# Dense gates of a routed expert layer from one-hot products: bf16 in three parts against rounded fp32 in two

## The chip, the cores and the metric

The kernel runs on one core of one Trainium2 chip. The metric is the device time of one execution in microseconds (us); the comparison goes by the median of several runs. The profile is of one execution, with a time of its own.

## The reference, cut to what matters

The kernel is a whole encoder block. What the change touches is the expert layer (PEER) at its end. Each of 512 tokens picks, for each of 8 heads, 16 experts out of 128 x 128, with a softmax gate on each:

```python
s_top, i_top = lax.top_k(s, PEER_TOPK)                    # two halves of 128 keys
cand = s_top[:, :, 0, :, None] + s_top[:, :, 1, None, :]
cand_idx = i_top[:, :, 0, :, None] * PEER_NKEYS + i_top[:, :, 1, None, :]
best_s, best_j = lax.top_k(cand.reshape(n, PEER_HEADS, -1), PEER_TOPK)
expert = jnp.take_along_axis(cand_idx.reshape(n, PEER_HEADS, -1), best_j, axis=-1)
gate = jax.nn.softmax(best_s, axis=-1)
h = jnp.einsum('nd,nhkd->nhk', xb, u[eb])
coef = gb * jax.nn.gelu(h, approximate=False)
out = jnp.einsum('nhk,nhkd->nd', coef, v[eb])
```

For 384 of the 512 tokens the kernel computes all 16384 experts densely and multiplies with a gate that is zero for experts that were not picked. So it needs, for each of these tokens, the dense 128 x 128 matrix of its gates: the sum over its 128 picks of gate x (one-hot of the first key) x (one-hot of the second key). The other 128 tokens fetch the rows of their picks instead.

## The kernel before, in words

The stages run one after the other, with a barrier of all engines between them: `project`, `attend`, `scan_chunks`, `join`, `route`, `experts`. The change lies in `route`.

`route` streams 104 weight tiles of 128 x 1024 fp32 from memory: 16 tiles of the query projection and 88 expert tiles (expert keys whose hidden values are computed early and parked in memory). Each tile is split in a high part (ScalarE, line 1669) and a low part (the difference), both written as fp32r, fp32 rounded for TensorE. GpSimd makes the low part for the first 56 tiles (line 1644), VectorE for the last 48 (`low`, line 1936). TensorE multiplies a tile in 24 products: 16 with the high part (line 1741), 8 with the low part (line 1745), each with 384 columns for an expert tile. ScalarE applies GELU (line 1675) and issues the store (line 1678).

Order of the stage: 48 tiles while VectorE ranks the scores (`rank`), then 8 tiles "between" (`BETWEEN`), in whose middle TensorE turns the picks over by transposes (line 1785) so that a token's 128 picks lie along the partitions; VectorE copies the three turned pieces (first key, second key, gate) out of PSUM (line 1908) and splits the gate into three bf16 parts (lines 1910 to 1916). Then come 24 lots of 16 tokens. A lot has two expert tiles and four "fours", each of 4 tokens. For a four, VectorE

- compares a count of 0 to 127 with the first key of each pick (line 1925, into `is_key`),
- compares it with the second key (line 1926, into `hot2`),
- multiplies `is_key` with each gate part (line 1929, into `hot1`).

TensorE then makes, for each of the 4 tokens, one product per gate part of 128 x 128 x 128, added up in PSUM (line 1798). ScalarE copies a four from PSUM into the lot (line 1714), and SP stores the lot, 1 MB, when its fours are copied. `hot1` and `hot2` are rings of `RING` = 4 fours: VectorE waits before a four until TensorE has done the four four places earlier (`four_done`).

Orders on the engines' queues within a lot n, all written out by hand:

- TensorE: expert tile, four 4n, four 4n+1, expert tile, four 4n+2, four 4n+3.
- VectorE: four 4n, four 4n+1, low half of the lot's second tile, four 4n+2, four 4n+3, low half of the next lot's first tile, one product of a gathered row (`dot_rows`, line 1969). Ahead of lot 0 stands the low half of its first tile.
- ScalarE: high half of the tile three ahead, GELU and store of the tile, two copies, and the same again.
- GpSimd: after its low halves, the gathers of 24 rows of the expert table, in a ring of 8.

Of the kernel before, what the change touches and what calls it, by code (L numbers as in the profile page):

```python
# [18 lines left out]
F32 = mybir.dt.float32  # L19
BF16 = mybir.dt.bfloat16  # L20
F32R = mybir.dt.float32r
U32 = mybir.dt.uint32
ALU = mybir.AluOpType
ACT = mybir.ActivationFunctionType
AX = mybir.AxisListType

P = 128
# [18 lines left out]
DENSE = SEQ - P  # L46
# [1489 lines left out]
def route(nc, a, g):  # L1536
# [4 lines left out]
    K = PEER_TOPK  # L1541
# [7 lines left out]
    FOUR = 4  # L1549
    FOURS = LOTS * LOT // FOUR  # L1550
    PARTS3 = 3
    RING = 4
    with ExitStack() as ctx:
# [5 lines left out]
        free = h1T.rearrange("p k t -> p (k t)")  # L1559
        act_out, qT = (free[:, 2048 + 1024 * x:3072 + 1024 * x].rearrange("p (j t) -> p j t", j=2) for x in range(2))  # L1560


        hot2 = sb("hot2", [P, RING, 2, P, 2], BF16)
        is_key = sb("is_key", [P, 2, 2, P, 2], BF16)
# [8 lines left out]
        gateT = sb("gateT", [P, DENSE])  # L1573

        gate_parts = sb("gate_parts", [P, FOURS, PARTS3, FOUR], BF16)
        picks_b = sb("picks_b", [P, 2, DENSE], BF16)
        small = sb("small", [P, NT * PEER_HEADS])
        count16, count128 = sb("count16", [P, K]), sb("count128", [P, P, 2], BF16)
# [8 lines left out]
        hot1 = sb("hot1", [P, RING, PARTS3, 2, P, 2], BF16)  # L1587
# [13 lines left out]
        gate_split, compared = sem("gate_split"), sem("compared")  # L1601
# [35 lines left out]
        @block.gpsimd  # L1637
        def _(pool):
            nc.gpsimd.iota(count16[:, :], [[1, K]], 0, 0, allow_small_or_imprecise_dtypes=True).then_inc(counted, 1)  # L1639
            nc.gpsimd.iota(count128[:, :, :], [[1, P], [0, 2]], 0, 0, allow_small_or_imprecise_dtypes=True).then_inc(counted, 1)  # L1640

            def low(s, j):
                pool.wait_ge(w_high, s + 1)
                nc.gpsimd.tensor_tensor(w_hl[:, j % RING, 1, :], staged[:, j % RING, :],  # L1644
                                        w_hl[:, j % RING, 0, :].bitcast(F32), ALU.subtract).then_inc(w_low, 1)

            with pool.Fori(0, BY_POOL // 8) as i:
                for j in range(8):
                    low(i * 8 + j, j)
            pool.wait_ge(gathering["picked"], 1)  # L1650
            for n in range(GATHERED_EARLY):
                gather_rows(nc, pool, a, gathering, n)

        @block.scalar
        def _(act):
# [50 lines left out]
            for j in range(BETWEEN):  # L1706
                expert(TOPK_TILES + j)
                if j == 1:
                    act.wait_ge(lowered, 1)
                    nc.scalar.activation(picks[:, 2], picks[:, 2], ACT.Exp).then_inc(raised, 1)  # L1710

# [18 lines left out]
        def _(pe):  # L1730
# [59 lines left out]
            def four(u):  # L1790

                q = u % 4
                if u >= 4:
                    pe.wait_ge(four_copied, u - 3)
                pe.wait_ge(hot_ready, u + 1)
                for n in range(FOUR):
                    for part in range(PARTS3):
                        last = nc.tensor.matmul(ps[:, 4 + q, P * n:P * (n + 1)], hot2[:, q, n // 2, :, n % 2],  # L1798
                                                hot1[:, q, part, n // 2, :, n % 2],
                                                start=(part == 0), stop=(part == PARTS3 - 1))  # L1800
                last.then_inc(four_done, 1)
# [8 lines left out]
        def _(dve):  # L1810
# [95 lines left out]
            for x in range(3):  # L1906
                dve.wait_ge(picks_turned, x + 1)
                v_.tensor_copy(gateT[:, :] if x == 2 else picks_b[:, x, :], ps[:, 4 + x, 0:DENSE]).then_inc(picks_copied, 1)
            dve.wait_ge(picks_copied, 3)
            by_four = gateT[:, :].rearrange("p (u n) -> p u n", n=FOUR)  # L1910
            for part in range(PARTS3):
                v_.tensor_copy(gate_parts[:, :, part, :], by_four).then_inc(gate_split, 1)
                dve.wait_ge(gate_split, 2 * part + 1)
                if part < PARTS3 - 1:
                    v_.tensor_tensor(by_four, by_four, gate_parts[:, :, part, :], ALU.subtract).then_inc(gate_split, 1)
                    dve.wait_ge(gate_split, 2 * part + 2)

            def four(u):

                r, now = u % RING, slice(FOUR * u, FOUR * (u + 1))  # L1920
                count = count128[:, :, :].unsqueeze(1).broadcast_to([P, 2, P, 2])
                pairs = lambda x: picks_b[:, x, now].rearrange("p (m n) -> p m n", n=2).unsqueeze(2).broadcast_to([P, 2, P, 2])
                if u >= RING:
                    dve.wait_ge(four_done, u - RING + 1)
                v_.tensor_tensor(is_key[:, u % 2], count, pairs(0), ALU.is_equal).then_inc(compared, 1)
                v_.tensor_tensor(hot2[:, r], count, pairs(1), ALU.is_equal)
                dve.wait_ge(compared, u + 1)
                part_pairs = gate_parts[:, u, :, :].rearrange("p c (m n) -> p (c m) n", n=2)
                v_.tensor_tensor(hot1[:, r].rearrange("p c m k n -> p (c m) k n"),
                                 is_key[:, u % 2].unsqueeze(1).broadcast_to([P, PARTS3, 2, P, 2]),  # L1930
                                 part_pairs.unsqueeze(2).broadcast_to([P, 2 * PARTS3, P, 2]), ALU.mult
# [368 lines left out]
```

## Time and profile before

| | |
|---|---|
| Time, median of 3 runs | 2092.43 us (2092.4 to 2100.97) |
| Profiled execution: its time, its span | 2092.4 us, 2090.7 us |
| Busy over the span: TensorE, VectorE | 91%, 74% |
| Busy over the span: ScalarE, GpSimd | 36%, 27% |
| Lots of `route`, first to last four on TensorE | 1067.33 to 1334.75 us |
| Mean granted TensorE clock over the span | 0.946 of full speed |

The profile names engines PE (TensorE products), PEld (TensorE weight loads, which overlap PE), DVE (VectorE), ACT (ScalarE), POOL (GpSimd) and SP (SyncE). L1929 is line 1929 of the kernel. Times are from the start of the span. Records of one engine may overlap the next by a little, since it is pipelined, so the cadence is read from starts and not from durations. "[0.21 <-PE ps L1798]" behind a row is idle time of that engine before it, and who ended it. A row with a count merges instructions of one kind in a row. DMA rows marked SPq or ACTq are issues of those queues.

### The profile page before, as it was taken

What the parts mean: (1) busy time and instruction counts of PE and PEld (TensorE: products, weight loads), DVE (VectorE), ACT (ScalarE), POOL (GpSimd) and SP (SyncE); (2) the same over time, 40 slices, a digit from 0 to 9 for tenths busy, and PEclk for the clock granted to TensorE, in tenths of its full rate; (3) what the DMA queues carried; (4) which work ended last, traced back from release to release, by engine and by line L of the source; (5) the groups of instructions that cost most, each with busy time, mean ns of one, the idle gap of its engine ahead of it and who ended that gap; (6) DMA issues with size and microseconds to landing.
All of it is one profiled execution on the core that took longest, in us unless ns stands there. A gap on an engine that the chain in (4) does not pass through costs nothing. (4 is left out here: it accounts for less than half of the span.)

```text
span 2090.7 us, 33958 instructions
## 1 busy us (share of the span) xinstructions
PE 1903.4 (91%) x13250; PEld 1622.2 (78%) x13250; DVE 1538.9 (74%) x2834; ACT 755.0 (36%) x1113; POOL 569.9 (27%) x395
## 2 busy tenths in 40 slices
PE   6989998879999879999499999579999999999996
PEld 4968876349874459999499999558888889999995
DVE  6278993414545369999978888368888887999998
ACT  3232454532220033433246656323333333333332
POOL 2322343000000045555221000112222225566660
PEclk9988998987999989999799999789999999999998
DMA  3211231010022044444277776599999998999992
GB/s 124 72 60 51 86 115 61 0 41 3 4 98 105 0 145 137 140 132 132 67 274 262 267 270 216 217 325 367 339 367 347 350 360 301 358 392 386 385 404 103
DMA packets 169686, 411.02 MB, mean 197 GB/s; under 512 B 13504, under 2 KB 85184, under 8 KB 166352
## 3 DMA queue, kind: packets, MB, share of 16 engines
q1 hardware_dynamic: 117712, 253.41, 35.2%
q0 software_dynamic: 36864, 134.23, 16.8%
q10 hardware_dynamic: 14976, 21.50, 2.8%
q8 instruction: 95, 1.56, 0.3%
q14 instruction: 39, 0.32, 0.0%
HBM read 360.33 MB, written 48.76 MB: 196 GB/s over the span
## 5 line engine op out<-in xcount | busy, mean ns | idle before, releaser
L2143 PE MATMUL ps<-v_hl,coef_hl 128*128 128x512 f32 x2304 | 535.9, 392 | 40.5 <-DVE coef_hl L2182 40.5
L2143 PEld LDWEIGHTS ps<-v_hl,coef_hl 128*128 128x128 f32 x2304 | 434.7, 189 | 131.4 <-DVE coef_hl L2182 42.0
L1741 PE MATMUL ps<-h_hl,w_hl 128*128 128x384 f32 (+1 forms) x1664 | 329.6, 350 | 8.7 <-DVE h_hl L1814 8.7
L1741 PEld LDWEIGHTS ps<-h_hl,w_hl 128*128 128x128 f32 x1664 | 294.8, 190 | 20.2 <-issue 9.1
L1959 POOL DMA_INDIRECT gathered_rows<-in_u_rows,pick_index x128 | 136.2, 1064 | 574.0 <-DVE pick_hidden L1969 465.3
L2087 ACT ACTIVATE v_hl<-v_staged 128x1024 fp32r<-128x1024 f32 x128 | 135.4, 1057 | 254.6 <-PE ps L2143 195.3
L2187 DVE TENSOR_TENSOR v_hl<-v_staged,v_hl 128x1024 fp32r<-128x1024 f32 x128 | 156.4, 1222 | 68.8 <-ACT v_hl L2087 68.8
L1959 POOL DMA_INDIRECT gathered_rows<-in_v,pick_index x128 | 176.0, 1375 | 105.6 <-DVE h_tok L1978 75.1
L1644 POOL TENSOR_TENSOR w_hl<-w_staged,w_hl 128x1024 fp32r<-128x1024 f32 x56 | 142.7, 2551 | 151.9 <-ACT w_hl L1669 151.6
L1978 DVE SCALAR_TENSOR_TENSOR h_tok<-gathered_rows,pick_hidden,h_tok 128x1024 f32<-128x1024 f32 x128 | 164.1, 1282 | 10.4 <-DVE h_tok L1978 0.5
L633 PE MATMUL ps<-hT_hl,w_hl 128*128 128x264 f32 (+1 forms) x1024 | 168.4, 323 | 0.0
L1745 PE MATMUL ps<-h_hl,w_hl 128*128 128x384 f32 (+1 forms) x832 | 168.1, 343 | 0.0
L633 PEld LDWEIGHTS ps<-hT_hl,w_hl 128*128 128x128 f32 x1024 | 150.9, 198 | 14.4 <-issue 2.8
L298 POOL TENSOR_TENSOR w_hl<-w_staged,w_hl 128x1024 fp32r<-128x1024 f32 x40 | 102.9, 2573 | 213.8 <-ACT w_hl L481 213.8
L1969 DVE CUSTOM_DVE_ANT_0 gathered_rows<-gathered_rows,h_tok 128x1024 f32<-128x1024 f32 x128 | 155.0, 1217 | 0.0
L1745 PEld LDWEIGHTS ps<-h_hl,w_hl 128*128 128x128 f32 x832 | 147.3, 188 | 5.0
L2093 ACT ACTIVATE coef_hl<-coef 128x384 fp32r<-128x384 f32 x128 | 65.7, 514 | 172.8 <-DVE coef L2178 172.8
L1669 ACT ACTIVATE w_hl<-w_staged 128x1024 fp32r<-128x1024 f32 x104 | 110.6, 1065 | 38.9 <-DMA w_staged<-in_stream 22.0
L2129 PE MATMUL ps<-h_hl,u_hl 128*128 128x384 f32 x640 | 118.4, 336 | 0.0
L2129 PEld LDWEIGHTS ps<-h_hl,u_hl 128*128 128x128 f32 x640 | 113.1, 188 | 3.1
L1639 POOL IOTA count<- 128x16 f32 x1 | 0.1, 149 | 398.3 <-POOLq L111 398.3
L1714 ACT ACTIVATE lot<-ps 128x512 f32<-128x512 f32 x96 | 95.9, 1105 | 19.9 <-PE ps L1798 19.9
(320 smaller groups left out, 2780.1 us busy)
## 6 DMA issues: line engine op xcount, KB each, us to landing
v_staged<-in_v SPq DMA_DIRECT2D x128, 512.0 KB
w_staged<-in_stream SPq DMA_DIRECT2D x104, 512.0 KB
dense_gates<-lot SPq DMA_DIRECT2D x24, 1024.0 KB
gates<-dense_gates SPq DMA_DIRECT2D x16, 1536.0 KB
w_staged<-in_w_in_t SPq DMA_DIRECT2D x40, 512.0 KB
h1T<-in_stream SPq DMA_DIRECT2D x40, 512.0 KB
parked_gelu<-h1T ACTq DMA_DIRECT2D x88, 192.0 KB, 2.5
coef<-parked_gelu SPq DMA_DIRECT2D x88, 192.0 KB
```

The source lines that it names most:

```text
L633: nc.tensor.matmul(banks[b], w_hl[:, j, 0, P * k:P * (k + 1)], hT_hl[:, part, k, lo:hi], start=(k == 0 and part == 0), stop=False)
L1644: nc.gpsimd.tensor_tensor(w_hl[:, j % RING, 1, :], staged[:, j % RING, :], w_hl[:, j % RING, 0, :].bitcast(F32), ALU.subtract).then_inc(w_ ...
L1669: nc.scalar.activation(w_hl[:, j % RING, 0, :], staged[:, j % RING, :], ACT.Copy).then_inc(w_high, 1)
L1741: nc.tensor.matmul(bank, w_hl[:, j % RING, 0, P * k:P * (k + 1)], h_hl[:, part, k, lo:hi], start=(k == 0 and part == 0), stop=False)
L1745: last = nc.tensor.matmul(bank, w_hl[:, j % RING, 1, P * k:P * (k + 1)], h_hl[:, 0, k, lo:hi], start=False, stop=(k == KD - 1))
L1959: nc.gpsimd.indirect_dma_start(gathering["rows"][:, slot, :], None, table, bass.IndirectOffsetOnAxis(gathering["index"][:, column:column + ...
L1969: nc.vector.tensor_tensor_reduce(rows, rows, h_tok[:, 0, :], 1.0, 0.0, ALU.mult, ALU.add, gathering["hidden"][:, n:n + 1]).then_inc(gather ...
L1978: nc.vector.scalar_tensor_tensor(h_tok[:, 0, :], gathering["rows"][:, slot, :], gathering["hidden"][:, pick:pick + 1], h_tok[:, 0, :], ALU ...
L2087: nc.scalar.activation(v_hl[:, k % HLS, 0, :], v_staged[:, k % STAGED, :], ACT.Copy).then_inc(v_high, 1)
L2129: nc.tensor.matmul(bank, u_hl[:, f % 2, 0, P * c:P * (c + 1)], h_hl[:, part, c, SEQ - DENSE:SEQ], start=(c == 0 and part == 0), stop=False)
L2143: last = nc.tensor.matmul(ps[:, 2 + 2 * t + half, :], coef_hl[:, k % HLS, c, P * t:P * (t + 1)], v_hl[:, k % HLS, v, 512 * half:512 * (hal ...
L2187: v_.tensor_tensor(v_hl[:, k % HLS, 1, :], v_staged[:, k % STAGED, :], v_hl[:, k % HLS, 0, :].bitcast(F32), ALU.subtract).then_inc(v_low, 1)
```

## The change

The three bf16 parts of the gate become two fp32r parts, high and low, and the one-hot tiles become fp32r too. `hot1` (3 parts) becomes `hot1_hl` (2 parts). The layout in pairs (`P, 2` innermost) is given up for a plain `[FOUR, P]`, so the key and the gate are now broadcast along the innermost dimension. A four has 8 products instead of 12. The high part of the gate is made by ScalarE, in its queue behind the tiles between, and VectorE waits for it (`gate_high`), subtracts and waits for that (`gate_low`) before its first low half. `is_key` moves into free room of `h1T`.

```diff
+        is_key = free[:, 0:2 * FOUR * P].rearrange("p (r n k) -> p r n k", r=2, n=FOUR)
-        hot2 = sb("hot2", [P, RING, 2, P, 2], BF16)
-        is_key = sb("is_key", [P, 2, 2, P, 2], BF16)
+        hot2 = sb("hot2", [P, RING, FOUR, P], F32R)
-        gateT = sb("gateT", [P, DENSE])
-        gate_parts = sb("gate_parts", [P, FOURS, PARTS3, FOUR], BF16)
-        picks_b = sb("picks_b", [P, 2, DENSE], BF16)
+        picksT = sb("picksT", [P, 3, DENSE])
+        gate_hl = sb("gate_hl", [P, 2, DENSE], F32R)
-        count16, count128 = sb("count16", [P, K]), sb("count128", [P, P, 2], BF16)
+        count16, count128 = sb("count16", [P, K]), sb("count128", [P, P])
-        hot1 = sb("hot1", [P, RING, PARTS3, 2, P, 2], BF16)
+        hot1_hl = sb("hot1_hl", [P, RING, 2, FOUR, P], F32R)
...
         # ScalarE, behind the loop over the tiles between
+            act.wait_ge(picks_copied, 3)
+            nc.scalar.activation(gate_hl[:, 0, :], picksT[:, 2, :], ACT.Copy).then_inc(gate_high, 1)
...
         # TensorE, in four(u)
-                    for part in range(PARTS3):
-                        last = nc.tensor.matmul(ps[:, 4 + q, P * n:P * (n + 1)], hot2[:, q, n // 2, :, n % 2],
-                                                hot1[:, q, part, n // 2, :, n % 2],
-                                                start=(part == 0), stop=(part == PARTS3 - 1))
+                    for part in range(2):
+                        last = nc.tensor.matmul(ps[:, 4 + q, P * n:P * (n + 1)], hot2[:, q, n, :],
+                                                hot1_hl[:, q, part, n, :], start=(part == 0), stop=(part == 1))
...
         # VectorE
-                v_.tensor_copy(gateT[:, :] if x == 2 else picks_b[:, x, :], ps[:, 4 + x, 0:DENSE]).then_inc(picks_copied, 1)
+                v_.tensor_copy(picksT[:, x, :], ps[:, 4 + x, 0:DENSE]).then_inc(picks_copied, 1)
             dve.wait_ge(picks_copied, 3)
-            by_four = gateT[:, :].rearrange("p (u n) -> p u n", n=FOUR)
-            for part in range(PARTS3):
-                v_.tensor_copy(gate_parts[:, :, part, :], by_four).then_inc(gate_split, 1)
-                dve.wait_ge(gate_split, 2 * part + 1)
-                if part < PARTS3 - 1:
-                    v_.tensor_tensor(by_four, by_four, gate_parts[:, :, part, :], ALU.subtract).then_inc(gate_split, 1)
-                    dve.wait_ge(gate_split, 2 * part + 2)
+            dve.wait_ge(gate_high, 1)
+            v_.tensor_tensor(gate_hl[:, 1, :], picksT[:, 2, :], gate_hl[:, 0, :].bitcast(F32), ALU.subtract
+                             ).then_inc(gate_low, 1)
+            dve.wait_ge(gate_low, 1)
...
-                v_.tensor_tensor(is_key[:, u % 2], count, pairs(0), ALU.is_equal).then_inc(compared, 1)
-                v_.tensor_tensor(hot2[:, r], count, pairs(1), ALU.is_equal)
+                v_.tensor_tensor(is_key[:, u % 2], count, picksT[:, 0, now].unsqueeze(2).broadcast_to([P, FOUR, P]),
+                                 ALU.is_equal).then_inc(compared, 1)
+                v_.tensor_tensor(hot2[:, r], count, picksT[:, 1, now].unsqueeze(2).broadcast_to([P, FOUR, P]), ALU.is_equal)
                 dve.wait_ge(compared, u + 1)
-                v_.tensor_tensor(hot1[:, r].rearrange("p c m k n -> p (c m) k n"),
-                                 is_key[:, u % 2].unsqueeze(1).broadcast_to([P, PARTS3, 2, P, 2]),
-                                 part_pairs.unsqueeze(2).broadcast_to([P, 2 * PARTS3, P, 2]), ALU.mult
+                v_.tensor_tensor(hot1_hl[:, r], is_key[:, u % 2].unsqueeze(1).broadcast_to([P, 2, FOUR, P]),
+                                 gate_hl[:, :, now].bitcast(F32).unsqueeze(3).broadcast_to([P, 2, FOUR, P]), ALU.mult
                                  ).then_inc(hot_ready, 1)
```

## Rows read from the trace of the kernel before

**Rows 1.** Busy time by engine over the lots; then PEclk, DMA share, GB/s.
```profile
1067.33:1334.75 267.42, 267.42 (x2281) 260.02 (x2280) 223.10 (x367) 159.75 (x187) 17.70 (x15) 1.00 0.70 241
```

**Rows 2.** Timeline of one lot: start, length, engine, line, operation.
```profile
1178.88 1.22 DVE L1936 TENSOR_TENSOR w_hl<-w_staged,w_hl 128x1024 fp32r<-128x1024 f32 x1
1180.01 1.22 DVE L1969 CUSTOM_DVE_ANT_0 gathered_rows<-gathered_rows,h_tok 128x1024 f32<-128x1024 f32 x1
1180.53 1.40 PEld L1798 LDWEIGHTS ps<-hot 128*128 128x128 bf16 x24 [0.16 <-issue]
1181.45 0.43 DVE L1925 TENSOR_TENSOR is_key<-count,picks_b 128x512 bf16<-128x512 bf16 x1 [0.21 <-PE ps L1798]
1181.79 0.42 DVE L1926 TENSOR_TENSOR hot<-count,picks_b 128x512 bf16<-128x512 bf16 x1
1181.89 2.76 PEld L1741 LDWEIGHTS ps<-h_hl,w_hl 128*128 128x128 f32 x16
1182.12 0.95 DVE L1929 TENSOR_TENSOR hot<-is_key,gate_parts 128x1536 bf16<-128x1536 bf16 x1
1182.99 0.42 DVE L1925 TENSOR_TENSOR is_key<-count,picks_b 128x512 bf16<-128x512 bf16 x1
...
1186.19 1.40 PEld L1798 LDWEIGHTS ps<-hot 128*128 128x128 bf16 x24 [0.16 <-issue]
1187.11 0.43 DVE L1925 TENSOR_TENSOR is_key<-count,picks_b 128x512 bf16<-128x512 bf16 x1 [1.36 <-PE ps L1798]
```

**Rows 3.** Groups by line in the lots: busy us, mean ns | idle before.
```profile
L1929 DVE TENSOR_TENSOR hot<-is_key,gate_parts 128x1536 bf16<-128x1536 bf16 x92 | 87.4, 950 | 0.0
L1798 PEld LDWEIGHTS ps<-hot 128*128 128x128 bf16 x1152 | 67.1, 97 | 7.5 <-issue 7.5
L1936 DVE TENSOR_TENSOR w_hl<-w_staged,w_hl 128x1024 fp32r<-128x1024 f32 x45 | 54.7, 1216 | 0.0
L1925 DVE TENSOR_TENSOR is_key<-count,picks_b 128x512 bf16<-128x512 bf16 x92 | 38.8, 421 | 40.3 <-PE ps L1798 40.3
L1926 DVE TENSOR_TENSOR hot<-count,picks_b 128x512 bf16<-128x512 bf16 x92 | 38.4, 417 | 0.0
```

**Rows 4.** Four-byte vector operations elsewhere, by line: ns min/median/max.
```profile
L1814 DVE TENSOR_TENSOR h_hl<-h1T,h_hl x8: 681/682/691, 753.3 to 757.5; 128x512 fp32r<-128x512 f32 x8
...
L1862 DVE TENSOR_TENSOR cand<-top x8: 1210/1212/1218, 795.7 to 1020.3; 128x1024 f32<-128x1024 f32 x8
...
L1876 DVE TENSOR_TENSOR is_place<-place,count x16: 1210/1226/3429, 806.6 to 1031.4; 128x1024 f32<-128x1024 f32 x16
```

**Rows 5.** Weight loads of 64 and of 128 fp32 columns, by line.
```profile
L1205 PEld LDWEIGHTS ps<-inv,low x256: 129/135/136, 498.7 to 597.0; 64*64 64x64 f32 x128
...
L1755 PEld LDWEIGHTS ps<-sub_keys,h1T x128: 187/192/192, 776.4 to 983.8; 128*128 128x128 f32 x128
```

**Rows 6.** Timelines of TensorE in two other stages, for the cadence of its products.
```profile
60.56 4.09 PE L633 MATMUL ps<-hT_hl,w_hl 128*128 128x264 f32 x32
64.49 2.12 PE L638 MATMUL ps<-hT_hl,w_hl 128*128 128x264 f32 x16
...
776.59 1.95 PE L1755 MATMUL ps<-sub_keys,h1T 128*128 x16
778.29 1.99 PE L1741 MATMUL ps<-h_hl,w_hl 128*128 128x384 f32 x10
```

**Rows 7.** Timeline ahead of the first lot.
```profile
1046.27 2.44 DVE L1912 CAST gate_parts<-gateT 128x384 bf16<-128x384 f32 x1
...
1053.02 1.23 DVE L1936 TENSOR_TENSOR w_hl<-w_staged,w_hl 128x1024 fp32r<-128x1024 f32 x1 [2.08 <-ACT w_hl L1669]
1063.37 0.49 ACT L1675 ACTIVATE h1T<-ps 128x384 f32<-128x384 f32 x1 [2.14 <-PE ps L1745]
1063.89 0.34 ACTq L1678 DMA_DIRECT2D parked_gelu<-h1T  x1
```

**Rows 8.** Timeline of TensorE's last four products.
```profile
1333.36 1.57 PE L1798 MATMUL ps<-hot 128*128 128x128 bf16 x24
```

More of the change, by code:

```diff
@@ L1550, in route @@
     FOURS = LOTS * LOT // FOUR
-    PARTS3 = 3
     RING = 4
@@ L1600, in route @@
             sem(n) for n in ("lowered", "raised", "gates_ready", "picks_turned", "picks_copied"))
-        gate_split, compared = sem("gate_split"), sem("compared")
+        gate_high, gate_low, compared = sem("gate_high"), sem("gate_low"), sem("compared")
         hot_ready, four_done, four_copied = sem("hot_ready"), sem("four_done"), sem("four_copied")
@@ L1639, in _ @@
             nc.gpsimd.iota(count16[:, :], [[1, K]], 0, 0, allow_small_or_imprecise_dtypes=True).then_inc(counted, 1)
-            nc.gpsimd.iota(count128[:, :, :], [[1, P], [0, 2]], 0, 0, allow_small_or_imprecise_dtypes=True).then_inc(counted, 1)
+            nc.gpsimd.iota(count128[:, :], [[1, P]], 0, 0, allow_small_or_imprecise_dtypes=True).then_inc(counted, 1)
             def low(s, j):
@@ L1918, in four @@
+            v_.tensor_tensor(gate_hl[:, 1, :], picksT[:, 2, :], gate_hl[:, 0, :].bitcast(F32), ALU.subtract
+                             ).then_inc(gate_low, 1)
+            dve.wait_ge(gate_low, 1)
             def four(u):
                 r, now = u % RING, slice(FOUR * u, FOUR * (u + 1))
-                count = count128[:, :, :].unsqueeze(1).broadcast_to([P, 2, P, 2])
-                pairs = lambda x: picks_b[:, x, now].rearrange("p (m n) -> p m n", n=2).unsqueeze(2).broadcast_to([P, 2, P, 2])
+                count = count128[:, :].unsqueeze(1).broadcast_to([P, FOUR, P])
@@ L1927, in four @@
                 dve.wait_ge(compared, u + 1)
-                part_pairs = gate_parts[:, u, :, :].rearrange("p c (m n) -> p (c m) n", n=2)
-                v_.tensor_tensor(hot1[:, r].rearrange("p c m k n -> p (c m) k n"),
-                                 is_key[:, u % 2].unsqueeze(1).broadcast_to([P, PARTS3, 2, P, 2]),
-                                 part_pairs.unsqueeze(2).broadcast_to([P, 2 * PARTS3, P, 2]), ALU.mult
+                v_.tensor_tensor(hot1_hl[:, r], is_key[:, u % 2].unsqueeze(1).broadcast_to([P, 2, FOUR, P]),
+                                 gate_hl[:, :, now].bitcast(F32).unsqueeze(3).broadcast_to([P, 2, FOUR, P]), ALU.mult
```

## Prediction

> **What bounds the kernel now.** I began with the page: its sum rows say where the engines are busy but not which of them sets the pace in the stretch that the diff touches, so I looked for the stretch itself. The loop of 24 lots runs from 1067.33 us, when the first one-hot product starts, to 1334.75. In it TensorE is busy for the whole stretch, VectorE for 83% of it, ScalarE for 60%, at full clock [rows 1]. The timeline of one lot shows the same as a cadence: a half lot is one expert tile (24 products of 384 columns) and two fours (24 products of 128 columns), and repeats after 5.66 us, for instance from 1180.53 to 1186.19. Weight loads of the tile start at 1181.89, those of the next fours at 1186.19 after a gap of 0.16, so the tile takes 4.14 us (172.5 ns a product) and the two fours 1.36 us (57 ns a product) [rows 2]. A lot is 11.32 us. VectorE waits for TensorE in every half lot, 0.21 and 1.36 us, because the ring of four hot tiles is full; TensorE waits for nobody [rows 2, 3]. So TensorE bounds this stage, and VectorE follows with a slack of 1.57 us in 11.32. That slack is the number on which the change depends.
>
> **VectorE, the term that decides.** One four is now 421 + 417 + 950 ns for 512, 512 and 1536 two-byte elements [rows 3]. Their successors start 0.34, 0.33 and 0.87 us later: each record overlaps the next by some 0.085 us, and a four has a cadence of 1.54 us [rows 2]. After the change it is 512, 512 and 1024 elements of four bytes. The trace has these: the four-byte operation on 512 elements takes 682 ns, on 1024 elements 1210 to 1218; with both operands broadcast (the candidate sums) it is 1212, and a comparison with an innermost broadcast has the same minimum, 1210 [rows 4]. The output type with rounding costs nothing extra, since the low half of a weight tile, written that way, takes 1216 [rows 3]. So the elements pass at 1.04 ns each instead of 0.52, and two thirds of the third operation's elements at twice the time is more. A four becomes 682 + 682 + 1216 = 2580 ns against 1788: +0.79 us, cadence 2.33.
>
> A lot on VectorE is four fours, two low halves at 1.13 (1178.88 to 1180.01) and a row product at 1.22. Now 6.16 + 2.26 + 1.22 = 9.64, plus 1.57 of waiting, leaves 0.11 of small gaps in 11.32. Then: 9.32 + 2.26 + 1.22 + 0.11 = 12.91 us. VectorE alone needs 1.59 us more per lot than the lot takes now.
>
> **TensorE, the term without a row.** The products fall from 12 to 8 a four, but become single-pass four-byte products with 128 moving columns, of which the trace has none. From below: such products with 264 and 384 columns come every 122.8 ns (32 in 3.93 us) and 172.5 ns, which is a column per 2.4 GHz clock plus 13 ns [rows 2, 6]; so 53.3 + 12.7 = 66 ns. From the middle: a weight load of 128 four-byte columns has a record of 188 to 192 ns, one of 64 columns 135, so 0.84 ns a column and 107 ns for 128 beside a fixed part; the two-byte load of 128 columns is 97 in all [rows 3, 5]. Behind 264 or more columns such a load is hidden, behind 128 it isn't. From above: the ordinary four-byte product of 128 columns gives two records, 106 ns apart (16 in 1.70 us), 213 ns a product [rows 5, 6]; with the 13 ns added, 226. I take 107, since the weight-load records are of the very type and width that the change uses, and an unhidden load is the only thing in them that differs from the longer products. The Trainium skill, TensorE: Matmul & The Clock Gate, section Weight-path perf modes, says that the fast weight load is on for 128 weights of any type but FP32; with that page's load of one column per 1.2 GHz cycle (section LDWEIGHTS) the load would be 107 ns, against 66 if one went by the longer products alone. The trace's 0.84 ns a column agrees with it, but no run of before shows the pair with 128 columns.
>
> A half lot on TensorE is then 4.14 + 0.16 + 16 products: 5.36 us with 66 ns, 6.01 with 107, 7.71 with 213, 7.92 with 226; a lot 10.7, 12.0, 15.4 or 15.8 us. Up to 107, and even at 120 (12.4), VectorE with 12.91 is the slower engine, and the price of a product doesn't enter the sum.
>
> **Start and end.** Removed are the five gate splits, from 1046.27 to the wait that ends at 1053.02. They are hidden: in that wait VectorE stands 2.08 us for ScalarE anyway [rows 7], so they return nothing. The three copies from PSUM stay. Added are one ScalarE copy of 384 elements and one subtraction on VectorE (384 elements: 682 less 128 x 1.04 = 0.55 us). The copy stands in ScalarE's queue behind the last tile of the eight between, whose GELU ends at 1063.86, its store's issue at 1064.2 [rows 7]; the copy ends near 1064.8 (0.5 us), the subtraction near 1065.5. Queued behind that wait on VectorE are the first low half, and all fours. TensorE's tile now waits for that low half: it wants it at 1067.33 - 0.16 - 1.38 (8 of 24 products) = 1065.8. The low half ends near 1066.7, TensorE loses some 0.9 us, and VectorE, which had its first four fours done before 1067, starts its first only at 1066.7. It thus loses its whole lead of four fours.
>
> From there VectorE runs without a stop: TensorE has finished each ring slot long before VectorE wants it again. 24 lots of 12.91 less the low half and the row product that stand behind the last four (2.35) end at 1066.7 + 309.8 - 2.35 = 1374.2. With 0.1 to finish, 0.9 for the last eight products and 0.2 of flush it is 1375.4, against 1334.9 now (1333.36 + 1.57) [rows 8]: +40.5 us. ScalarE's work per lot is unchanged, 6.9 us of 12.9, and so is what follows the stage: the same buffers and the same first transfers, later by that much. Nothing of the later stages runs ahead, as they begin behind a barrier. The profiled execution took 2092.4 us, 1.7 more than its span and equal to the median of the runs; 2092.4 + 40.5 = 2133.
>
> **Rivals.**
> A. Products with 128 columns take the four-pass rate, 213 to 226 ns. For it: the only four-byte products with such short rows show it. Against: those are of the plain type and leave two records each, while the rounded type leaves one at 264 columns and above. TensorE is then the bound: fours 0 and 1 are ready at 1069.0 and 1071.4, the second ends at 1073.1, and 47 half lots of 7.71 to 7.92 follow: 1435.5 to 1445.3, so +100 to +110, 2193 to 2203 us. The Trainium skill, FP8 and Floating Point Precision, section TensorE Precision Notes, keeps four passes for true FP32 and lets the reduced form be truncated on reading, which speaks against this rival; no row has the case.
> B. An exposed weight load and the product don't overlap: 107 + 53 = 160 ns. A half lot is 6.86; 1072.7 + 47 x 6.86 = 1395.1, +60, 2152 us. Against it: the plain product's records, with loads of the same 188 to 192 ns, are only 106 apart [rows 5, 6].
> C. Faster: the four-byte vector operations keep a cadence under the TensorE lot, and TensorE gains from 8 products at 66 ns instead of 12 at 57. It decides when a four is under 1.93 us (11.32 less 3.48 and 0.11, over four); then a lot falls towards 10.72, 24 x 0.6 = 14 us less, 2078. Against it are all rows of group 4, which give 2.33.
> D. The slack covers it all: no change. The same point, 1.93 us a four, with 107 ns on TensorE would make lots of 12.0 and so still +16; only a price between 66 and 85 ns gives no change.
>
> **How the numbers follow.** My forecast (VectorE bound, any TensorE price up to 120 ns) gets 0.62, B 0.08, A 0.25, C 0.03, D 0.02. The forecast's own range is 2124 to 2142: 0.4 us a lot either way for gaps on VectorE. Leaving out A would leave out a quarter, so the range reaches to it: 2124 to 2204. A measurement of this kernel can tell about 0.5% (10 us) from nothing; by these cases 0.03 faster, 0.02 within it, 0.95 slower.
>
> **What would show it.** In the lots: comparisons of about 682 ns twice and a multiplication of 1216, VectorE busy without waits for the products, lots of 12.9 us; TensorE waiting for the hot tiles; 8 products a four at 107 ns, weight loads of 188 to 192. The first comparison near 1066.7, the last product near 1375. Rival A shows products over 200 ns apart and VectorE still waiting; B 160. I am wrong if the four-byte comparison with its stride-zero operands is not one element per 1.04 ns, or if TensorE, idle for a moment in each lot, loses its granted clock, as the rows at 1.00 don't show [rows 1].

## The result

| | median | lowest to highest | runs |
|---|---|---|---|
| before | 2092.41 us | 2091.73 to 2100.97 | 4 |
| changed | 2131.38 us | 2130.43 to 2132.12 | 4 |

The change costs 39.0 us: the ratio is 1.0176, with a 95% interval of 1.015 to 1.0203. A second set of the same kernel, run on one chip with three of the experiments, gave 2129.12 us against 2092.47, ratio 1.017 (1.0129 to 1.0212). 2133 us was forecast, slower.

The profiled execution of the changed kernel took 2135.26 us, span 2133.5, some 4 us over its median. A shift of 6.1 us is there before `route` has begun (the first low half of its activations starts at 759.4 us, at 753.3 in the profile of before [rows 4]), in stages whose code is unchanged. So I compare `route` from that instruction on: to the start of the last product it takes 581.4 us before and 618.6 after, 37.2 more. From there to the end of the span it is 756.0 and 755.5 us. The whole of the change lies in `route`. A second profiled execution of the changed kernel has the same 618.6 us there (754.8 to 1373.4).

### The profile page after: what moved, and what is told of

The parts are those of the page before. It is cut to its first block and busy times, and to the rows that moved or that the text cites. A ratio compares the mean times of both kernels' runs of the same rounds, so it can differ in the third digit from the quotient of the medians.

```text
span 2133.5 us, 33188 instructions
## 1 busy us (share of the span) xinstructions
PE 1929.4 (90%) x12866; PEld 1648.7 (77%) x12866; DVE 1608.0 (75%) x2830; ACT 757.5 (36%) x1114; POOL 567.8 (27%) x395
## 5 line engine op out<-in xcount | busy, mean ns | idle before, releaser
L1922 DVE TENSOR_TENSOR hot_hl<-h1T,gate_hl 128x1024 fp32r<-128x1024 f32 x96 | 117.2, 1220 | 0.0
```

Of the source, the lines that this page charges most:

```text
L1922: v_.tensor_tensor(hot1_hl[:, r], is_key[:, u % 2].unsqueeze(1).broadcast_to([P, 2, FOUR, P]), gate_hl[:, :, now].bitcast(F32).unsqueeze(3 ...
```

## The profile after

Busy time by engine from the first four to the last (columns as in [rows 1]: PE, PEld, DVE, ACT, POOL, then the granted clock, DMA share, GB/s):

```profile
1075.01:1378.31 303.30, 288.75 (x1896) 286.23 (x1896) 303.08 (x380) 161.38 (x186) 18.33 (x16) 0.99 0.62 214
```

[Rows 1] had TensorE busy for the whole of 267.42 us and VectorE for 223.10. Now VectorE is busy for the whole of 303.30 and TensorE for 288.75. The bound has changed engines.

The groups by line in the lots (busy us, mean ns, idle time before and its releaser), the answers to [rows 3]:

```profile
L1922 DVE TENSOR_TENSOR hot_hl<-h1T,gate_hl 128x1024 fp32r<-128x1024 f32 x96 | 117.2, 1220 | 0.0
L1796 PE MATMUL ps<-hot_hl,hot 128*128 128x128 f32 x768 | 95.8, 273 | 15.2 <-DVE hot_hl L1922 15.2
L1796 PEld LDWEIGHTS ps<-hot_hl,hot 128*128 128x128 f32 x768 | 94.6, 192 | 17.9 <-issue 15.6 <-DVE hot_hl L1922 2.4
...
L1918 DVE TENSOR_TENSOR h1T<-count,picksT 128x512 f32<-128x512 f32 x96 | 66.0, 687 | 0.0
L1920 DVE TENSOR_TENSOR hot<-count,picksT 128x512 fp32r<-128x512 f32 x96 | 65.9, 687 | 0.0
L1928 DVE TENSOR_TENSOR w_hl<-w_staged,w_hl 128x1024 fp32r<-128x1024 f32 x48 | 58.6, 1220 | 0.0
```

The waits have changed sides. The comparison `is_key` waited 40.3 us for products [rows 3] and now waits 0.0; the products wait 15.2 us for `hot1_hl`. (The name h1T in these rows is where `is_key` lies now.) A four on VectorE is 687 + 687 + 1220 = 2594 ns, where 421 + 417 + 950 = 1788 stood [rows 3].

One lot of the timeline, from VectorE's and the weight loads' side (start, length), the answer to [rows 2]:

```profile
1180.55 0.68 DVE L1918 TENSOR_TENSOR h1T<-count,picksT 128x512 f32<-128x512 f32 x1
...
1182.89 0.68 DVE L1918 TENSOR_TENSOR h1T<-count,picksT 128x512 f32<-128x512 f32 x1
...
1184.61 1.92 PEld L1796 LDWEIGHTS ps<-hot_hl,hot 128*128 128x128 f32 x16
...
1185.23 1.22 DVE L1928 TENSOR_TENSOR w_hl<-w_staged,w_hl 128x1024 fp32r<-128x1024 f32 x1
...
1186.37 1.22 DVE L1961 CUSTOM_DVE_ANT_0 gathered_rows<-gathered_rows,h_tok 128x1024 f32<-128x1024 f32 x1
1186.45 2.73 PEld L1739 LDWEIGHTS ps<-h_hl,w_hl 128*128 128x128 f32 x16
...
1187.51 0.08 DVE L1961 DVE_READ_ACCUMULATOR2_ANT pick_hidden<- 128x1 f32 x1
1187.51 0.69 DVE L1918 TENSOR_TENSOR h1T<-count,picksT 128x512 f32<-128x512 f32 x1
...
1192.39 0.97 PEld L1796 LDWEIGHTS ps<-hot_hl,hot 128*128 128x128 f32 x8 [0.80 <-issue]
1192.42 1.08 PE L1796 MATMUL ps<-hot_hl,hot 128*128 128x128 f32 x8 [0.69 <-DVE hot_hl L1922]
...
1193.33 0.68 DVE L1918 TENSOR_TENSOR h1T<-count,picksT 128x512 f32<-128x512 f32 x1
```

The same place in the lot is reached at 1180.55 and 1193.33: a lot is 12.78 us (11.32 before). A four takes 2.34 (1180.55 to 1182.89), and nothing on VectorE has idle time ahead of it. TensorE waits once a lot, 0.69 us before the second four. Sixteen products of two fours take 1.84 us (1184.61 to 1186.45, load to load), 115 ns each where twelve and twelve took 57 each.

Ahead of the first lot:

```profile
1070.16 0.53 ACT L1708 ACTIVATE gate_hl<-picksT 128x384 fp32r<-128x384 f32 x1 [0.41 <-ACT h1T L1671]
...
1070.79 0.56 DVE L1908 TENSOR_TENSOR gate_hl<-picksT,gate_hl 128x384 fp32r<-128x384 f32 x1 [18.61 <-ACT gate_hl L1708]
1071.39 1.23 DVE L1928 TENSOR_TENSOR w_hl<-w_staged,w_hl 128x1024 fp32r<-128x1024 f32 x1
1072.53 0.69 DVE L1918 TENSOR_TENSOR h1T<-count,picksT 128x512 f32<-128x512 f32 x1
1072.66 1.34 PEld L1743 LDWEIGHTS ps<-h_hl,w_hl 128*128 128x128 f32 x8 [0.99 <-DVE w_hl L1928]
```

VectorE stands idle for 18.61 us for the gate's high part, and TensorE's weight loads for the tile then wait 0.99 us for its low half. The first comparison starts at 1072.53, less the shift of 6.1 at 1066.4.

TensorE's granted clock just behind these waits, and the tile that ran then:

```profile
1078.90:1082.00 3.10, 3.10 (x11) 3.10 (x11) 3.10 (x6) 1.94 (x2) 0.00 (x0) 0.50 0.54 169
...
1090.00:1378.30 288.30, 274.98 (x1827) 272.61 (x1825) 288.09 (x362) 155.00 (x179) 17.19 (x15) 1.00 0.64 219
```
```profile
1077.35 1.91 PE L1796 MATMUL ps<-hot_hl,hot 128*128 128x128 f32 x8 [1.23 <-DVE hot_hl L1922]
1079.06 5.39 PE L1739 MATMUL ps<-h_hl,w_hl 128*128 128x384 f32 x16
1084.28 1.58 PE L1743 MATMUL ps<-h_hl,w_hl 128*128 128x384 f32 x8
```

TensorE's products had waited 0.67, 0.68 and 1.23 us within 6 us. Behind that the granted clock read 0.50, the level of 1.2 GHz, and the 16 products of a tile took 5.22 us (1079.06 to 1084.28) where they take 2.83 at 1.00 (1180.56 to 1183.39). It cost nothing here, since VectorE had no idle time in these lots. From 1090 on, with one wait of 0.69 us a lot, the clock read 1.00.

## The experiments

All but the two with bf16 parts are edits of the changed kernel. The profiled lots are the sharper measure, since the timed runs of one kernel spread by up to 17 us in some sets. In the profiled executions the stages ahead of `route`, whose code is the same in all of them, end at different times: the first low half of the activations starts between 747.9 and 759.4 us.

### What bounds the lots: fewer products, less multiplication, more products

`high_products_only`:

```diff
-                    for part in range(2):
+                    for part in range(1):
                         last = nc.tensor.matmul(ps[:, 4 + q, P * n:P * (n + 1)], hot2[:, q, n, :],
-                                                hot1_hl[:, q, part, n, :], start=(part == 0), stop=(part == 1))
+                                                hot1_hl[:, q, part, n, :], start=True, stop=True)
```

> The changed kernel with four products a four instead of eight: only the high gate part is multiplied in, the low part is made on VectorE but left out of the sum. If VectorE bounds the lots (my theory), nothing moves: about 2131 us, lots still 12.8 us, TensorE only waits longer. If TensorE with its products (115 ns apart in the trace of after) sets the pace, 96 x 4 x 0.115 = 44 us go: about 2087.

Busy time over its lots:

```profile
1061.70:1364.50 302.80, 258.84 (x1512) 253.28 (x1512) 302.80 (x379) 161.83 (x186) 18.32 (x16) 0.95 0.62 214
```

TensorE is busy for 29.9 us less (288.75 to 258.84) and the lots are as long as before: 302.8 us against 303.3. (The products taken out were worth some 44 us at 115 ns each. TensorE's mean granted clock in these lots is 0.95 instead of 0.99, which makes an estimate of 0.04 x 303 = 12 us by which the rest took longer.) VectorE is busy in all of them. From the first low half (747.9) to the last product (1364.0) it is 616.1 us, 618.6 in the changed kernel. The time is 2134.26 us (2121.17 to 2138.21), ratio 1.0215 (1.0187 to 1.0243): no gain. That half of TensorE's new products weigh nothing is shown. The ratio even lies above that of the changed kernel, while the profiled execution is the fastest of the set, with the earliest start of `route` of all (747.9 us). The three slower ones have a lower mean clock (0.940 and 0.935 twice, against 0.943); they were not profiled, so the cause stays open.

`high_multiply_only`:

```diff
-                v_.tensor_tensor(hot1_hl[:, r], is_key[:, u % 2].unsqueeze(1).broadcast_to([P, 2, FOUR, P]),
-                                 gate_hl[:, :, now].bitcast(F32).unsqueeze(3).broadcast_to([P, 2, FOUR, P]), ALU.mult
+                v_.tensor_tensor(hot1_hl[:, r, 0], is_key[:, u % 2],
+                                 gate_hl[:, 0, now].bitcast(F32).unsqueeze(2).broadcast_to([P, FOUR, P]), ALU.mult
...
-                                                hot1_hl[:, q, part, n, :], start=(part == 0), stop=(part == 1))
+                                                hot1_hl[:, q, 0, n, :], start=(part == 0), stop=(part == 1))
```

> The changed kernel with VectorE multiplying the high part alone (512 elements instead of 1024); the eight products stay, both with the high part, so the low part is left out. VectorE's four falls from 2.33 to 1.80 us, its lot from 12.8 to 10.7. If VectorE bounds the lots, they fall until TensorE does, 2 x (4.14 + 0.16 + 16 x 0.115) = 12.3 us: 24 x 0.5 = 12 us less, about 2119. If TensorE already bounds them, no change, 2131.

Busy time over its lots, and weight loads of one half lot in its timeline:

```profile
1062.60:1346.00 283.40, 281.71 (x1896) 281.43 (x1896) 254.96 (x380) 160.97 (x188) 18.85 (x16) 1.00 0.66 230
```
```profile
1182.40 1.92 PEld L1796 LDWEIGHTS ps<-hot_hl,hot 128*128 128x128 f32 x16
1184.24 2.73 PEld L1739 LDWEIGHTS ps<-h_hl,w_hl 128*128 128x128 f32 x16
```

The time falls to 2107.81 us (2100.49 to 2117.09), ratio 1.0094 (1.0058 to 1.0131). 512 elements less a four, on VectorE alone, take back half of the change by the medians and 23.3 of its 37.2 us in the trace. That is the direction expected with VectorE as the bound, and the rival (TensorE bound) is excluded. The size was wrong: 12 us were expected, 1.0176 to 1.0094 is 17, and in the trace (749.4 to 1344.7, 595.3 us) it is 23.3. TensorE bounds these lots, but at a half lot of 5.94 us, not the 6.14 of the expectation: 1.84 for the products and 4.11 for the tile, without the 0.16 us that stood ahead of the fours in [rows 2]. In this kernel 24 x (12.78 - 5.94 x 2) = 21.6 us is the VectorE part of the change, and 24 x (11.88 - 11.32) = 13 us the part that TensorE would charge if VectorE cost nothing.

`twelve_products`:

```diff
-                    for part in range(2):
+                    for x, part in enumerate((0, 1, 1)):
                         last = nc.tensor.matmul(ps[:, 4 + q, P * n:P * (n + 1)], hot2[:, q, n, :],
-                                                hot1_hl[:, q, part, n, :], start=(part == 0), stop=(part == 1))
+                                                hot1_hl[:, q, part, n, :], start=(x == 0), stop=(x == 2))
```

> The changed kernel with 12 products a four, the low part multiplied in twice. It doubles as a test of TensorE's price and of where it would take over. With 115 ns a product, as the trace of after has it, a half lot on TensorE is 4.11 + 24 x 0.115 = 6.87 us, a lot 13.7, above VectorE's 12.8: 24 x 0.96 = 23 us more than the changed kernel. At 107 ns it is 14 us more, at 66 ns nothing.

Busy time over its lots, and its weight loads:

```profile
1065.70:1392.00 326.30, 324.61 (x2280) 324.33 (x2280) 304.45 (x380) 165.46 (x187) 18.33 (x16) 1.00 0.58 199
```
```profile
1182.94 2.82 PEld L1796 LDWEIGHTS ps<-hot_hl,hot 128*128 128x128 f32 x24
1185.67 2.73 PEld L1739 LDWEIGHTS ps<-h_hl,w_hl 128*128 128x128 f32 x16
...
1189.78 2.82 PEld L1796 LDWEIGHTS ps<-hot_hl,hot 128*128 128x128 f32 x24
```

2152.26 us against 2129.12 for the changed kernel on the same chip: +23.1, as expected. In the trace, from the first low half (752.0) to the last product (1390.8), it is 20.2 more. Half lots are 6.84 us (1182.94 to 1189.78), 24 products take 2.73 (114 ns each), and TensorE is again busy nearly from end to end. The two engines cross at (6.39 - 4.11) / 0.114 = 20 products a half lot, 10 a four (6.39 is half of VectorE's lot).

### Why such a product costs 112 to 115 ns

`wide_products` (first) and `narrow_weights` (second), one run each:

```diff
                 for n in range(FOUR):
-                    for part in range(2):
-                        last = nc.tensor.matmul(ps[:, 4 + q, P * n:P * (n + 1)], hot2[:, q, n, :],
-                                                hot1_hl[:, q, part, n, :], start=(part == 0), stop=(part == 1))
+                    last = nc.tensor.matmul(ps[:, 4 + q, 2 * P * (n % 2):2 * P * (n % 2 + 1)], hot2[:, q, n, :],
+                                            hot1_hl[:, q, n // 2, 2 * (n % 2):2 * (n % 2) + 2, :], start=True, stop=True)
```
```diff
-                        last = nc.tensor.matmul(ps[:, 4 + q, P * n:P * (n + 1)], hot2[:, q, n, :],
+                        last = nc.tensor.matmul(ps[0:64, 4 + q, P * n:P * (n + 1)], hot2[:, q, n, 0:64],
```

> The changed kernel with four products of 256 columns a four instead of eight of 128 (two tokens' halves side by side, so the sums over the parts are left out). A look at the cadence in the trace. If a product of 128 columns is bound by its weight load, one of 256 costs about the same, 107 to 120 ns, and two fours take 0.95 us instead of 1.84. If the moving columns set the price at 0.9 ns each, one of 256 takes 230 ns and two fours stay at 1.84. The lots stay at 12.8 us in both cases, VectorE being the bound.

> The changed kernel with weight loads of 64 columns instead of 128 (keys 64 to 127 of the second half are left out); still 8 products of 128 moving columns. If the weight load binds, the cadence falls from 115 ns to that of the moving columns, 53 + 13 = 66 ns, and two fours take about 1.06 us. If the moving columns bind, it stays at 115. The lots stay at 12.8 us.

One four in the timeline of `wide_products`, and one in that of `narrow_weights`:

```profile
1191.07 0.61 PE L1795 MATMUL ps<-hot_hl,hot 128*128 128x256 f32 x4
```
```profile
1188.20 0.64 PE L1796 MATMUL ps<-hot_hl,hot 128*64 128x128 f32 x8
```

A merged row runs from the first start to the last end, so the mean cadence, the time from one start to the next, is its length less one record, over the count less one. With 256 moving columns (a record is 279 ns) it is (610 - 279) / 3 = 110 ns; with 64 weight columns (record 223) it is (640 - 223) / 7 = 60 ns. In the changed kernel the product of 128 by 128 (record 274) stands at (1000 - 274) / 7 = 104 ns in a group of eight, 1.00 us long, and at (1900 - 274) / 15 = 108 in a group of 16. These two means are low because the second product of such a group starts only 57 ns after the first; the eight further products of the longer group cost (1900 - 1000) / 8 = 112 ns each. Over all lots the median from start to start is 112 ns with 128 by 128, 118 with 256 moving columns and 60 with 64 weight columns. So twice the moving columns cost at most some 6 ns, and half the weight columns save about 50. The load of 128 four-byte weight columns sets the price, as the middle estimate had it. With 64 weight columns the 60 ns are close to the 57 of the bf16 product, which has the same 128 moving columns, so there the load need no longer be what sets it. Both kernels took what the changed one takes (2128.81 and 2125.58 us, one run each), since VectorE sets the lots.

### The start: the gate's high part made earlier

```diff
             for j in range(BETWEEN):
...
+                if j == 3:
+                    act.wait_ge(picks_copied, 3)
+                    nc.scalar.activation(gate_hl[:, 0, :], picksT[:, 2, :], ACT.Copy).then_inc(gate_high, 1)
-            act.wait_ge(picks_copied, 3)
-            nc.scalar.activation(gate_hl[:, 0, :], picksT[:, 2, :], ACT.Copy).then_inc(gate_high, 1)
```

> The changed kernel with ScalarE's copy of the gate's high part moved ahead, right behind the fourth tile between instead of behind the eighth. My step on the start: VectorE makes its first four fours before TensorE wants them, and starts the fifth when the first is done, some 11 us earlier than now (1068.3 instead of 1066.6 + 12.8, in times of the profile of before); being the bound it keeps that: about 2120.5 us. Rival: the lead is used up in waits on the ring or is hidden by TensorE's tiles, less than 2 us of gain, 2130.

Its timeline, VectorE:

```profile
1043.52 0.56 DVE L1909 TENSOR_TENSOR gate_hl<-picksT,gate_hl 128x384 fp32r<-128x384 f32 x1 [0.67 <-ACT gate_hl L1709]
1048.92 1.23 DVE L1929 TENSOR_TENSOR w_hl<-w_staged,w_hl 128x1024 fp32r<-128x1024 f32 x1 [4.85 <-ACT w_hl L1665]
1050.07 0.69 DVE L1919 TENSOR_TENSOR h1T<-count,picksT 128x512 f32<-128x512 f32 x1
...
1064.28 0.69 DVE L1919 TENSOR_TENSOR h1T<-count,picksT 128x512 f32<-128x512 f32 x1 [1.32 <-PE ps L1797]
```

The wait of 18.61 us is 0.67. VectorE has four fours ready, waits once for the ring (1.32 us), and then keeps its lead as the bound. From the first low half (751.3) to the last product (1357.1) it is 605.8 us: 12.8 less than the changed kernel. 2115.3 us, ratio 1.0123 (1.01 to 1.0145) where the changed kernel had 1.0176 and 1.017: about 10 us. So the place of one ScalarE copy of 0.53 us carries a quarter to a third of the whole change.

### The number of products without the change of type

```diff
 (in the kernel before)
-    PARTS3 = 3
+    PARTS3 = 2
```

> The kernel before with two bf16 parts of the gate instead of three (the third, the last 8 bits of the gate, is left out): the saving in the number of products alone, without the change of type. TensorE bounds the lots there, so each half lot should lose 8 products of 57 ns: 48 x 0.45 = 22 us less, about 2071. VectorE's four falls to 1.27 us. Rival: the transfers (DMA busy 0.70 to 0.79 of the lots) or ScalarE's copies stop the fall; then 2075 to 2092.

> The kernel before with two bf16 parts instead of three, once more and in more rounds, since its first time had an interval of 11 us: 48 half lots of 5.19 instead of 5.66 us are 22.6 us less, a ratio of 0.989.

Weight loads in the timeline of the second set:

```profile
1180.08 0.93 PEld L1798 LDWEIGHTS ps<-hot 128*128 128x128 bf16 x16 [0.16 <-issue]
...
1185.28 0.93 PEld L1798 LDWEIGHTS ps<-hot 128*128 128x128 bf16 x16 [0.16 <-issue]
```

A half lot is 5.20 us. The first set gave a ratio of 0.9909 (0.9883 to 0.9935), the second 0.9889 (0.9864 to 0.9914), 2068.09 us against 2091.76. In the traces, from the first low half to the last product, it is 22.5 us less than before in the first set (756.6 to 1315.5) and 17.8 in the second (752.0 to 1315.6). In the second, TensorE's weight loads stood three times for the high half of a tile, once for 2.27 us:

```profile
1214.45 2.75 PEld L1741 LDWEIGHTS ps<-h_hl,w_hl 128*128 128x128 f32 x16 [2.27 <-ACT w_hl L1669]
```

The three are 4.8 us, and ScalarE, which makes the high halves, waited 57.0 us in 21 waits for transfers of the weight tiles. So the rival of the expectation, the transfers, begins to bind. The eight products a four that the change wanted are worth 18 to 23 us, if they keep the two-byte type. (VectorE multiplies 512 elements less a four too, but it had slack already.) This version beats both kernels; what it gives up is the third part of the gate, so that the gate has the 16 leading bits of its fraction instead of 24.

### Can VectorE get a part of it back?

`bf16_is_key` makes the first comparison in pairs and in bf16, as before, and multiplies in two instructions:

```diff
+                pairs = keys_b[:, now].rearrange("p (m n) -> p m n", n=2).unsqueeze(2).broadcast_to([P, 2, P, 2])
+                v_.tensor_tensor(is_key[:, u % 2], count_b[:, :, :].unsqueeze(1).broadcast_to([P, 2, P, 2]), pairs,
+                                 ALU.is_equal).then_inc(compared, 1)
...
+                for c in range(2):
+                    last = v_.tensor_tensor(hot1_hl[:, r, c].rearrange("p (m n) k -> p m k n", n=2), is_key[:, u % 2],
+                                            gate_hl[:, c, now].bitcast(F32).rearrange("p (m n) -> p m n", n=2).unsqueeze(2)
+                                            .broadcast_to([P, 2, P, 2]), ALU.mult)
+                last.then_inc(hot_ready, 1)
```

> The changed kernel with the first comparison in bf16 and in pairs, as before, and the multiplication in two instructions of 512 elements that read it beside the fp32 gate. VectorE's four: 0.34 + 0.60 + 1.20 = 2.14 us instead of 2.33, its lot 12.0 against TensorE's 11.9: some 18 us less than the changed kernel, 20 to 21 over the kernel before. If VectorE's time isn't what sets the lots, nothing changes. If an operation that mixes two-byte and four-byte operands costs more than 1.04 ns an element, less comes back.

It was a miss: 2171.03 us, ratio 1.038 (1.0347 to 1.0412), 42 us slower than the changed kernel. The comparison cost 422 ns as wanted, the multiplications 1089 each instead of the 682 that a four-byte operation on 512 elements takes. Two things had come together in them, mixed operand types and a write with 512 bytes between neighbouring elements, and two further kernels took them apart: `mixed_plain` only makes `is_key` bf16, `paired_fp32` only takes the paired layout, all in fp32.

```diff
 (mixed_plain)
-        is_key = free[:, 0:2 * FOUR * P].rearrange("p (r n k) -> p r n k", r=2, n=FOUR)
+        is_key = free[:, 0:FOUR * P].bitcast(BF16).rearrange("p (r n k) -> p r n k", r=2, n=FOUR)
```
```diff
 (paired_fp32)
-        is_key = free[:, 0:2 * FOUR * P].rearrange("p (r n k) -> p r n k", r=2, n=FOUR)
+        is_key = free[:, 0:2 * FOUR * P].rearrange("p (r m k n) -> p r m k n", r=2, m=2, n=2)
...
+                paired = lambda x: x.rearrange("p (m n) -> p m n", n=2).unsqueeze(2).broadcast_to([P, 2, P, 2])
+                v_.tensor_tensor(is_key[:, u % 2], count128[:, :].unsqueeze(1).unsqueeze(3).broadcast_to([P, 2, P, 2]),
+                                 paired(picksT[:, 0, now]), ALU.is_equal).then_inc(compared, 1)
...
+                for c in range(2):
+                    last = v_.tensor_tensor(hot1_hl[:, r, c].rearrange("p (m n) k -> p m k n", n=2), is_key[:, u % 2],
+                                            paired(gate_hl[:, c, now].bitcast(F32)), ALU.mult)
+                last.then_inc(hot_ready, 1)
```

> The changed kernel with is_key written as bf16 and everything else as it is: the multiplication reads a bf16 and an fp32 operand, in the plain layout. It separates the two things that came together in bf16_is_key, whose multiplications of 512 elements took 1089 ns instead of 682. If mixing two-byte and four-byte operands is what costs (1.84 ns an element), the multiplication takes some 2030 ns, a lot 3.3 us more, the kernel 78 us more than the changed one: about 2208. If the paired layout was the cause, it stays at 1216 ns and the kernel at 2130.

> The changed kernel with is_key in fp32 but in pairs, and the multiplication in two instructions that write with 512 bytes between neighbouring elements. If that write pattern is what made the 1089 ns, they take 1089 each here too, a four 3.0 us, and the kernel some 65 us more than the changed one, about 2195. If mixing the types was the cause, they take 682 ns each and the kernel is 6 us slower than the changed one, for the extra instruction: about 2136.

The multiplication in `bf16_is_key`, in `mixed_plain` and in `paired_fp32` (ns min/median/max, first and last start):

```profile
L1926 DVE TENSOR_TENSOR hot_hl<-h1T,gate_hl x192: 1031/1087/1152, 1063.2 to 1411.9; 128x512 fp32r<-128x512 bf16 x192
```
```profile
L1922 DVE TENSOR_TENSOR hot_hl<-h1T,gate_hl x96: 1215/1222/1228, 1064.1 to 1366.1; 128x1024 fp32r<-128x1024 bf16 x96
```
```profile
L1924 DVE TENSOR_TENSOR hot_hl<-h1T,gate_hl x192: 1045/1112/1209, 1072.8 to 1441.3; 128x512 fp32r<-128x512 f32 x192
```

Mixing costs nothing (1222 ns for 1024 elements, 2124.99 us). The layout is the cause: 1112 ns for 512 elements in pure fp32, 2199.16 us, one run each. And of the layout it is the write. The first comparison of `paired_fp32` reads in the same pairs but writes element by element in a row, and it costs what the plain second comparison beside it costs:

```profile
L1919 DVE TENSOR_TENSOR h1T<-count,picksT 128x512 f32<-128x512 f32 x75 | 53.1, 708 | 0.0
L1921 DVE TENSOR_TENSOR hot<-count,picksT 128x512 fp32r<-128x512 f32 x75 | 52.9, 706 | 0.0
...
1181.56 2.02 DVE L1924 TENSOR_TENSOR hot_hl<-h1T,gate_hl 128x512 fp32r<-128x512 f32 x2
1183.42 0.68 DVE L1919 TENSOR_TENSOR h1T<-count,picksT 128x512 f32<-128x512 f32 x1
```

The records overstate it a little: two multiplications take 1.86 us from start to start (1181.56 to 1183.42), 0.93 each. The slower two are changes on VectorE alone, and the end moved by their size: a four takes 2.77 us in `bf16_is_key` and 3.06 in `paired_fp32` instead of 2.34, so 96 x 0.43 = 41 and 96 x 0.72 = 69 us were to come, and 42 and 70 came (2171.03 and 2199.16 against 2129.12; in the traces, from the first low half to the last product, 45 and 66, and in the first of them VectorE also waited 4.9 us for a gathered row). That is two more signs of VectorE as the bound.

## Why the prediction was right, by its own steps

- **TensorE bounds the lots before, VectorE after.** Right. Taking TensorE work out of the changed kernel gained nothing, taking VectorE work out gained at once, and the idle time went over from one to the other.
- **A four on VectorE of 682 + 682 + 1216 ns.** Measured 687, 687, 1220, with a cadence of 2.34 us (2.33 forecast). The rows of other operations with the same element count and broadcast operands held for the new ones.
- **A lot of 12.91 us.** 12.78. The term that was mis-sized is the rest: the row product costs 1.14 (1186.37 to 1187.51), not 1.22, and the 0.11 us of gaps are gone, which fits that they stood beside waits for TensorE that no longer happen. 24 x 0.13 = 3.1 us is nearly all of the 3.3 by which the forecast for the stage was high (40.5 against 37.2).
- **The start.** First comparison forecast near 1066.7, found at 1066.4 after taking off the shift; TensorE's wait for the low half forecast at 0.9, found at 0.99 on the weight loads. The loss of the lead was folded into the sum; by itself it is 10 to 13 us, by `gate_copy_early`.
- **The removed gate splits return nothing.** Consistent with the trace, where VectorE waits for the gate's high part in their place, longer than they took; no run tried it by itself.
- **107 ns a product.** The cadence is 112, and 115 with the change of tile counted in. By the Trainium skill, TensorE: Matmul & The Clock Gate, section LDWEIGHTS, a weight load takes its number of columns over 1.2 in ns, whatever the rows, which makes an estimate of 107 ns for 128 columns. The runs come near it: 112 ns with 128 moving columns and 118 with 256, against 60 with 64 weight columns. With 66 ns the forecast time would have been the same, but not `twelve_products`.
- **Rival A (four passes, 213 to 226 ns) and B (160 ns)** are excluded by the same cadence. (The plain product's two records, from which A took its 213, stand (1950 - 275) / 15 = 112 ns apart in the 16 of [rows 6], with records of 275 ns. The 106 came from counting up to the next tile, whose first product starts 30 ns behind the last of them. And 112 is the very cadence of the changed kernel's products with loads of the same width, so the 213 may be a price of loads and not of passes; no run tried it.) **Rival C** needed a four under 1.93 us on VectorE; `high_multiply_only`, with 1.80, shows where it leads: not to a gain, since TensorE's price rose too. **Rival D** is excluded: the slack of 1.57 us a lot didn't cover 4 x 0.8.
- **The clock** read 1.00 of 2.4 GHz from 1090 us to the end of the lots, with a wait of 0.69 us a lot. The sign of being wrong that the prediction named, a clock lost in idle moments, did come once, in the first lot (0.50 from 1078.9 to 1082.0), and again with four products a four, where the lots' mean read 0.95. The lots didn't get longer either time, as VectorE set them.

The forecast of +40.5 us stands against +39.0 between the medians: 3.3 us too much in the stage, and 1.8 us that the medians show beside the 37.2 of the profiled stage, less than what one execution differs from the next. The two partly cancel: that the total came within 1.5 us is luck to that extent, while the terms were right to 3.3.

## What to carry to other kernels

Before trading more two-byte products for fewer four-byte ones, count the engine that prepares the operands: here four products a four were saved on the engine with the load, 2048 four-byte elements replaced 2560 two-byte ones on the other, and the second number decided. A small hidden copy behind a queue can cost many times its length when its consumer becomes the bound, so after a change of bound look again at everything that starts late. And the saving in products was real, 18 to 23 us, as long as the type stayed.

## What the runs showed of the hardware that was not expected

- A product of fp32r with 128 weight columns costs 112 ns with 128 moving columns and 118 with 256, and 60 ns with 64 weight columns and 128 moving ones. The bf16 product of 128 by 128 costs 57.
- A VectorE operation that writes fp32 with 512 bytes between neighbouring elements took 1112 ns for 512 elements by its record and 0.93 us from start to start, where a contiguous write of 512 elements takes 687 ns and 0.60 us (1180.55 to 1181.15 in the changed kernel). That is 0.33 us more, 0.6 ns an element. Reading in the same pairs cost nothing (708 ns against 706), and reading a bf16 beside an fp32 operand cost nothing (1222 against 1220).
- Three waits of TensorE of 0.67 to 1.23 us within 6 us were followed by a granted clock of 0.50 (1078.9 to 1082.0); single waits of 0.69 us every 12.78 us left it at 1.00.
